# One decoder layer on one core: a norm weight spread by TensorE, two turns moved by a slot, two sample pieces moved, and the last sums divided among three engines

## The reference

```
h = RMSNorm(x) * norm_mix_pre
rq, rk, rv, rg, aq, ak, av, gr, ga = split(h @ w_in)
ret = retention(rotary(rq), rotary(rk), rv), per-head norm, times silu(rg)
att = dilated window attention in 3 groups over aq, ak, av (samples: over a cache)
mix = (sigmoid(gr) * (ret @ w_branch_ret) + sigmoid(ga) * (att @ w_branch_attn)) @ w_out
x = x + RMSNorm(mix) * norm_mix_post
f = (gelu(conv(h2 @ w_up)[g]) * conv(h2 @ w_up)[v]) @ w_down
y = x + RMSNorm(f) * norm_ffn_post
```

## Time and profile before

| what | value |
|---|---|
| runs | 1020.61, 1021.45 (median), 1021.92 us |
| the profiled execution | 1019.37 us, its span 1017.6 us |
| PE busy | 987.1 us, 97% of the span |
| DVE, ACT, POOL busy | 550.6, 380.0, 180.6 us |
| mean granted clock of TensorE | 0.994 |
| first product of a block | at 12.97 us |

### The profile page before, as it was taken

The page is one execution under the profiler, slowest core; times in us unless marked ns, Lnnn a source line. Parts: engine busy times, 40 slices in busy tenths (PEclk is TensorE's granted clock), DMA queues, the critical chain, the costliest instruction groups (busy, mean ns, idle before and its releaser), DMA issues.

```text
span 1017.6 us, 20374 instructions
## 1 busy us (share of the span) xinstructions
PE 987.1 (97%) x7774; PEld 877.5 (86%) x7774; DVE 550.6 (54%) x898; ACT 380.0 (37%) x836; POOL 180.6 (18%) x365
## 2 busy tenths in 40 slices
PE   6999999999999999999999889999999999999997
PEld 4777787779999999998887679999999999877775
DVE  5355225435367888773155576666666666422226
ACT  6333222441543423333133744444444443212313
POOL 2102004034161344445110001000010000000100
PEclk9999999999999999999999999999999999999999
DMA  6734444546796676769534324545545554221323
GB/s 240 275 121 153 167 174 166 189 153 207 257 300 220 194 234 203 240 198 320 187 120 137 123 76 156 179 172 167 188 170 174 165 176 143 84 83 63 120 83 117
DMA packets 40465, 175.36 MB, mean 172 GB/s; under 512 B 6936, under 2 KB 7384, under 8 KB 38864
## 3 DMA queue, kind: packets, MB, share of 16 engines
q1 hardware_dynamic: 25616, 125.78, 35.9%
q0 software_dynamic: 14784, 48.65, 15.2%
HBM read 164.40 MB, written 54.05 MB: 215 GB/s over the span
## 4 chain that ended last, share of the span: by engine, by line
PE 84%; DVE 8%; DMA 3%; ACT 2%; issue 2%; POOL 0%; SPq 0%; DVEq 0%; ACTq 0%
PE bank L1339 10%; PE bank L1341 9%; PE bank L1340 9%; PE bank L1847 9%; PE bank L1848 9%; PE bank L1849 9%; PE bank L1421 6%; PE bank L1425 5%; PE bank L1424 5%; PE bank L1358 2%; PE bank L1321 2%; DMA wraw<-in_weights 1%; DMA qbc<-sample_queries 1%; PE bank L1754 1%; DVE wlo L1932 1%
## 5 line engine op out<-in xcount | busy, mean ns | idle before, releaser
L1932 DVE TENSOR_TENSOR wlo<-wraw,whi 128x1024 fp32r<-128x1024 f32 x89 | 108.8, 1222 | 285.7 <-ACT whi L834 285.5
L834 ACT ACTIVATE whi<-wraw 128x1024 fp32r<-128x1024 f32 x91 | 96.3, 1058 | 318.5 <-PE bank L1341 204.9
L1847 PE MATMUL bank<-T1h,whi 128*128 128x288 f32 (+1 forms) x704 | 202.5, 288 | 3.1 <-DVE T1l L1942 1.7
L1848 PE MATMUL bank<-T1l,whi 128*128 128x288 f32 (+1 forms) x704 | 203.6, 289 | 0.0
L1849 PE MATMUL bank<-T1h,wlo 128*128 128x288 f32 (+1 forms) x704 | 203.1, 288 | 0.0
L1847 PEld LDWEIGHTS bank<-T1h,whi 128*128 128x128 f32 x704 | 133.0, 189 | 3.8 <-issue 1.9
L1848 PEld LDWEIGHTS bank<-T1l,whi 128*128 128x128 f32 x704 | 132.7, 189 | 0.0
L1849 PEld LDWEIGHTS bank<-T1h,wlo 128*128 128x128 f32 x704 | 132.3, 188 | 0.0
L1339 PE MATMUL bank<-whi,T1h 128*128 128x512 f32 (+1 forms) x288 | 114.0, 396 | 0.5 <-DVE T1l L1942 0.3
L1421 PE MATMUL bank<-T1h,whi 128*128 128x272 f32 x384 | 113.4, 295 | 0.0
L1425 PE MATMUL bank<-T1h,wlo 128*128 128x272 f32 x384 | 111.0, 289 | 0.0
(11 more groups left out here) (306 smaller groups left out, 1817.6 us busy)
## 6 DMA issues: line engine op xcount, KB each, us to landing
wraw<-in_weights SPq DMA_DIRECT2D x142, 512.0 KB, 3.7
out_s_kv_g<-in_cache_kv_g SPq DMA_DIRECT2D x64, 511.0 KB
qbc<-sample_queries POOLq DMA_DIRECT2D x48, 256.0 KB, 4.8
kvk<-in_cache_kv_g POOLq DMA_DIRECT2D x32, 256.0 KB, 4.0
kvv<-in_cache_kv_g POOLq DMA_DIRECT2D x16, 512.0 KB, 8.0
out_s_kv_g<-in_cache_kv_g SPq DMA_DIRECT2D x16, 508.0 KB
S<-in_state_ret POOLq DMA_DIRECT2D x16, 256.0 KB, 3.3
out_s_ret<-S POOLq DMA_DIRECT2D x16, 256.0 KB, 6.3
```

What stands on the lines that cost most here:

```text
L834: nc.scalar.activation(w_halves(s)[0], wraw[:, s % 2, :], ACT.Copy).then_inc(w_hi, 1)
L1847: mm(dst, Wh, T1h[:, k, c], start=k == 0, stop=False)
L1848: mm(dst, Wh, T1l[:, k, c], start=False, stop=False)
L1932: v.tensor_tensor(lo, wraw[:, s % 2, :], hi.bitcast(F), ALU.subtract).then_inc(w_lo, 1)
```

## The change

Four edits. (1) The norm weight is loaded as one row `grow` of 4 KB. PE multiplies a column of ones with it, two products of 512 columns in fp32 into banks 0 and 1. DVE copies these into `gpre`, and POOL, ahead of its two subtractions, waits for the products, since `grow` and `ones` lie where `wlo` will be. (2) `TURN_STEP` puts the turns of blocks 1 and 2 behind slot 2 rather than slot 1, on PE, ACT and DVE. (3) Two sample pieces go from the last two slots of the output gate to the first two of the retention gate; POOL now waits for output-gate slot 15 before it loads the near values. (4) For the first three tiles of the end, ACT scales the first half-row and POOL adds the residual, DVE does the second half alone.

```
-        sp.dma_start(gpre[:], a["norm_mix_pre"].broadcast_to([128, D])).then_inc(gpre_in, 16)
+        sp.dma_start(grow[0:1, :], a["norm_mix_pre"]).then_inc(grow_in, 16)
...
+        nc.gpsimd.memset(ones[0:1, :], 1.0).then_inc(ones_ready, 1)
...
+        pool.wait_ge(gain_full, 1)
         for j in range(2):
             pool.wait_ge(w_hi, j + 1)
...
+        pe.wait_ge(ones_ready, 1)
+        pe.wait_ge(grow_in, 16)
+        for half in range(2):
+            last = mm(P[half][:, :], ones[0:1, :], grow[0:1, 512 * half:512 * half + 512], start=True, stop=True)
+        last.then_inc(gain_full, 1)
         pe.wait_ge(ident_in, 16)
...
-        dve.wait_ge(gpre_in, 16)
+        dve.wait_ge(gain_full, 1)
+        for half in range(2):
+            v.tensor_copy(gpre[:, 512 * half:512 * half + 512], P[half][:, :]).then_inc(gpre_in, 1)
+        dve.wait_ge(gpre_in, 2)
...
+TURN_STEP = {1: 2, 2: 2, 5: 1, 6: 1, 7: 1}
...
-                turned = s == 1 and bi in (1, 2, 5, 6, 7)
+                turned = s == TURN_STEP.get(bi)
...
-                if bi in (1, 2) and s == 1:
+                if bi in (1, 2) and s == TURN_STEP[bi]:
                     turn_block(bi - 1)
...
-                if s == 1 and bi in (1, 2, 5, 6, 7):
+                if s == TURN_STEP.get(bi):
                     turn_evac(bi - 1, 1)
                     turn_evac(bi - 1, 3)
...
-PIECES_RG = 8 * (1,)
-PIECES_GB = 8 * (3, 2)
+PIECES_RG = (2, 2, 1, 1, 1, 1, 1, 1)
+PIECES_GB = 7 * (3, 2) + (2, 1)
...
         pool.wait_ge(s_step, 48)
+        pool.wait_ge(w_used, S_GB + 16)
         load_near_values(0)
-        pool.wait_ge(w_used, S_GB + 16)
...
+SHARED_LAST = 3
...
+        for p, i in enumerate(LAST_ORDER[:SHARED_LAST]):
+            r = rows(i)
+            pool.wait_ge(y_scaled, p + 1)
+            nc.gpsimd.tensor_tensor(fo[0:r, i, 0:512], fo[0:r, i, 0:512], xo[0:r, i, 0:512], ALU.add).then_inc(y_first, 1)
...
+                if 0 < p <= SHARED_LAST:
+                    i = LAST_ORDER[p - 1]
+                    r = rows(i)
+                    act.wait_ge(y_rs, p)
+                    nc.scalar.activation(x[0:r, i, 0:512], x[0:r, i, 0:512], ACT.Copy, scale=rs_n[0:r, at_ + i:at_ + i + 1]
+                                         ).then_inc(y_scaled, 1)
...
-            step(v.reciprocal(rs, rt_n[0:r, 10 + i:11 + i]))
-            for half in range(2):
+            v.reciprocal(rs, rt_n[0:r, 10 + i:11 + i]).then_inc(y_rs, 1)
+            dve.wait_ge(y_rs, p + 1)
+            for half in (1,) if p < SHARED_LAST else (1, 0):
```

More of the change, by code:

```diff
@@ L299, in build_layer @@
     gpre = sb("gpre", ATT + 5120, [128, D])
+    grow, ones = sb("gain_row", 13312 + SLOT, [128, D]), sb("ones", 13312, [128, 128])
     xn = sb("xn", ATT + 6144, [128, 2, D])
@@ L423, in build_layer @@
     x_again = [sem(f"x_again{i}") for i in range(TILES)]
-    ident_in = sem("ident_in")
+    ident_in, grow_in, ones_ready, gain_full = sem("ident_in"), sem("grow_in"), sem("ones_ready"), sem("gain_full")
     ca_in, cr_in, gpre_in, convp_in = sem("ca_in"), sem("cr_in"), sem("gpre_in"), sem("convp_in")
@@ L462, in build_layer @@
     half_sq, half_bias, x_scaled = sem("half_sq"), sem("half_bias"), sem("x_scaled")
-    y_sq, y_rt, y_ready = sem("y_sq"), sem("y_rt"), sem("y_ready")
+    y_sq, y_rt, y_rs, y_scaled = sem("y_sq"), sem("y_rt"), sem("y_rs"), sem("y_scaled")
+    y_first, y_ready = sem("y_first"), sem("y_ready")
     y_out = sem("y_out")
@@ L586, in _ @@
             dst = o["y_prompt"][0, 128 * i:128 * i + 128, :] if i < 4 else o["y_sample"].rearrange("b t d -> (b t) d")
-            parts = ((0, 512), (512, 1024)) if p == TILES - 1 else ((0, 1024),)
-            for c0, c1 in parts:
-                sp.wait_ge(y_ready, 2 * p + c1 // 512)
+            parts = ((512, 1024), (0, 512)) if p == TILES - 1 else ((0, 1024),)
+            for n, (c0, c1) in enumerate(parts):
+                if p < SHARED_LAST:
+                    sp.wait_ge(y_first, p + 1)
+                    sp.wait_ge(y_ready, p + 1)
+                else:
+                    sp.wait_ge(y_ready, 2 * p + 2 - SHARED_LAST - (len(parts) - 1 - n))
                 sp.dma_start(dst[:, c0:c1], fo[0:rows(i), i, c0:c1]).then_inc(y_out, 16)
```

## The result

The changed kernel took 1024.37 us (median of 19 runs, 1021.82 to 1027.34), the kernel before on the same chips 1020.40 us (19 runs): ratio 1.0043, 95% interval 1.0035 to 1.0051. It is slower by 0.43%, about 4 us. The forecast was 1024.7, and slower by over 0.2% the likeliest case. The total is right, but several of its terms are not, and a part of the agreement is luck.

The account below looks back on a forecast made before the run. PE was 97% busy, so only its waits, start and end counted. Terms +2.4 + 0.1 - 1.6 + 3.5 - 1.1 = +3.3 gave 1022.7 from the profiled 1019.37; adding its 2.1 us under the median gave 1024.7, range 1020.0 to 1027.4.

Parts of the forecast that it names:

- forecast +2.4: Start: the chain of row, two PE products and two DVE copies delays `xn`, costing 2.4 us.
- upper bound of 3.1: Start: the loss if all of the delay of `gpre` is carried to PE's products, +3.1 us.
- second rival: Start costs little, +0.9 us or less, by PE's fast pace and an early row; total 1023.2; chance 0.14.
- forecast +0.1: Turns of blocks 1 and 2: the wait on turned tiles is exchanged for one on `wlo`; +0.1 us for both.
- third rival: Turns of blocks 1 and 2 gain what they seem to, -2.6 us; total 1022.0; chance 0.06.
- forecast -1.6 and +3.5: Sample pieces: the `sTk` wait at the output gate's end goes, -1.6 us; PE's turn in the retention gate moves +3.5.
- the landing is later: Retention gate: piece 3's queries land 6.1 us after issue, at 301.25, later than DVE's work would reach it, 300.4.
- 4 us which the forecast named as a sign: Retention gate: the forecast would be wrong if piece 3's queries land within 4 us.
- forecast's own lower bound: Retention gate: the work alone, without a later landing of queries, delays PE's turn by +2.7 us.
- first rival: Retention gate: piece 3 holds nobody, so the 3.5 us go; total 1021.2, not slower; chance 0.20.
- forecast -1.07: End: without one half-sum in each of three tiles DVE finishes near 1014.03 instead of 1015.10, -1.07 us.
- fourth rival: End: POOL's third sum holds a DVE half-sum by up to 1.25 us; +0.8 us, total 1025.5; chance 0.10.

Follow-up runs that it names:

- experiment with the row first: Kernel before with only the norm-weight row change, the row's load issued ahead of x tile 0; ratio 0.9981 (0.9968 to 0.9994).
- Edit 2 alone: Kernel before with only the turns of blocks 1 and 2 moved behind slot 2; ratio 1.0013 (1.0000 to 1.0025).
- the split inside the rotation: Kernel before with the moved turns, DVE making `wlo` of slots 6 and 10 between third and fourth rotated tile; ratio 0.9971.
- edit 3 alone: Kernel before with only the two sample pieces moved to the first two retention-gate slots; ratio 1.0007 (0.9997 to 1.0017).
- two slots later: Kernel before with the two sample pieces moved to retention-gate slots 4 and 5 instead of 0 and 1; ratio 0.9971 (0.9957 to 0.9985).
- edit 4 alone: Kernel before with only the end's first three tiles shared with ACT and POOL; ratio 0.9986 (0.9974 to 0.9998).
- Sharing two tiles: Kernel before with only the end's change, two tiles shared with ACT and POOL instead of three; ratio 0.9990 (0.9979 to 1.0002).
- changed kernel with the row first: The whole changed kernel with the norm-weight row's load issued ahead of x tile 0; 1020.98 us, ratio 1.0003 to the kernel before.

## Why the prediction was right, and where not

The number was right: +3.3 forecast, +4.0 measured between medians, sign and range as forecast. A part of that is luck. The terms were counted from one profiled execution to another, and between the two profiles they come to +7.2: nearly every term of loss was too small, and the gain at the end too large. The 2.1 us that were then added, the distance of that execution from the median of three runs, are 1.0 by the median of 19. The four edits measured alone add up to +0.21 + 0.13 + 0.07 - 0.14 = +0.27%, about 2.8 us and uncertain by some 2.4, which agrees with 4.0 and is too coarse to check the sum.

Two of the forecast's bounds do not follow from their own terms: 2.4 less 1.1 or 1.6 is +1.3 or +0.8, not +0.9 for either, and 1024.7 + 1.8 + 0.7 is 1027.2, not 1027.4. Neither matters for the outcome.

**Edit 1, forecast +2.4.** The size is right and its making is not. Measured: ratio 1.0021, 2.1 us; by the sample rows' products 2.7 us against the mean of the old starts. The row landed at 4.6 (4.4 forecast), the products took 3.75 us (3.3), the first `xn` began at 9.93 (9.3 to 9.6), all near. But the first block product came at 16.18, outside the 14.5 to 15.3, and 3.2 us behind that of before, just past the upper bound of 3.1. The missing piece is the second `xn`: I gave it 1.48 us with its reciprocal, but its delay pushed it onto POOL's subtraction. The row for it was in the earlier trace rows, 1.94 us for 1.28, and I used it at the end of the kernel and not at the start. The experiment with the row first removes the overlap and the delay together, so their shares are read from the traces, not from a run that parts them. The forecast had POOL's part end near 11.3; it ended at 10.51 + 2.92 = 13.43, and the second `xn`, begun at 11.32, ran into it.

The second rival (the row near 3.3 by the Trainium skill, "DMA: Bandwidth & Descriptors", "Anatomy of one DMA") was wrong as placed: behind the 512 KB of x tile 0 the row landed with it. Alone in front it was in use 1.56 us after its issue at 0.74, somewhat less than that section's fixed cost of about 2 us; the section gives it for transfers that GpSimd issues, and this row went by SP, so the two need not agree. Nor did the queue become shorter by what the forecast said: with 4 KB in place of 512 KB, x tile 1 was squared at 7.73 and 7.93. In the seven profiles with the old start that was at 7.70 (the kernel before) and at 8.16 to 8.44 (the other six), 8.19 on average, so the tile came about 0.4 us sooner and not 1.7. Weight slot 0 was rounded at 9.32 in after, against 9.08 before; the forecast had that start near 7.4.

**Edit 2, forecast +0.1.** Shown right in mechanism: two waits of 1.5 us on `wlo` for two of 1.3 on the turned tiles. The size is +0.43 for each block, by the times at which PE starts the same products in the two traces. Of that 0.27 is that five tiles' turns took 2.37 us and not 2.1; the rest is not resolved. Edit 2 alone gave +1.3 us with an interval from 0 to 2.6. The third rival (a gain of 2.6) fell, and the run with the split inside the rotation shows what it lacked.

**Edit 3, forecast -1.6 and +3.5.** The gain at the gate's end is there: the wait on `sTk` is gone, 1.8 us by the same products. At the front the step that failed is "the landing is later". Piece 3's queries, issued at 299.75, landed 3.7 us later and not 6.1, at 303.45, which is 1.5 us before the piece began (304.98). That is within the 4 us which the forecast named as a sign that it would be wrong. It was wrong about what holds the chain; the hold itself came all the same, from the work. The wait for queries fell on piece 1 (0.91 us, about the 1 us given). The work alone bound it, the forecast's own lower bound: `w_split` started at 306.31 instead of 299.13, 7.2 us later, while PE came to its turn only 4.5 us later (310.17 - 2.96 = 307.21 against 303.00 - 0.29 = 302.71). The 2.7 us between them are what PE waits more: 2.96 for 0.29. What made the total larger again is a term that I did not have: the clock fell to 0.50 behind the wait, for 1.5 us more by the times of the same products. 2.7 + 1.5 = 4.2 us in these two profiles, against 3.5. That the two lie near each other is accident. The first rival, that piece 3 holds nobody, is refuted by the wait of 2.9 us in the run of edit 3 alone and by its absence two slots later.

**Edit 4, forecast -1.07.** Half of it came: 3.12 - 2.64 = 0.48 us, and the traces of three and of two shared tiles agree. The times alone (0.2 to 2.6 us for edit 4 alone) could not tell 0.5 from 1.07. The fourth rival's mechanism was there, since the half-sums took 2.15 us instead of 1.41. By the Trainium skill, "SBUF — State Buffer", "Who interferes with whom", a DVE instruction with two SBUF inputs and a POOL one that reads SBUF contend; the traces agree here and in the start (3.18 us for 1.28). Its price over the forecast is 2.64 - 2.05 = 0.6 us, and in after's trace that is all that was missing: half-sums of 1.41 us would have ended at 1017.90 + 1.41 = 1019.31, just as the last tile's square was done (1019.33), and they ended at 1020.05. Sharing two tiles does not reach the 2.05 (2.56), because DVE then carries the third tile's other half. Whether three sums by an engine that doesn't block DVE would reach 2.05 wasn't tried.

**The sum of the two profiles.** After less before, by the times at which PE starts the same products: start +3.4, first weight loads +0.3, turns 2 x 0.43, retention gate +4.2, one slot of the output gate +0.5, `sTk` -1.8, `hn`'s turns +0.35, end -0.5. Together 7.3, where the spans differ by 7.2. The medians differ by 3.2 less. Of the 19 runs of after, the 12 with a mean granted clock of 0.995 or more took 1024.0 us on average and the 7 with 0.994 or less 1026.2, so a part of that gap goes with the clock, and another 0.6 us with the lucky start of before's profile. The rest is open.

## What to carry to other kernels

When a wait is removed, write down what is late next and amend that too: three of these edits were a small loss or nothing as made, and a gain of 2 to 3 us once one thing more was moved. Put a tiny transfer that heads a chain ahead of the large ones, not behind. Before delaying a DVE instruction with two SBUF inputs, look at what POOL will be doing at its new time; and a wait of 0.3 us on a chain is a warning that the chain has no slack.

## What the hardware did that was not expected

- A PE wait of 2.2 to 3.0 us in the middle of dense work was followed by a granted clock of 0.50 for 2 us and more, in after, in edit 3 alone and in the changed kernel with the row first. Where the wait was 0.3 us at the same place the clock stayed at 1.00. The wait's price was half again as large as its row says, or more: by the stretches at most 1.7 us was lost behind each.
- The length of a wait does not settle this by itself. During or behind the wait of 3.1 us on `hn`, near 585 us, the clock fell to 0.50 in all ten profiles that have that wait, the kernel before among them; 1.7 us were lost in four (edit 2 alone, edit 4 alone, edit 1 with the row first, edit 3 two slots later) and 3.4 us in six. Behind the wait on `sTk` it fell, with 1.7 us lost, in the three profiles of edit 1, edit 2 and edit 4 alone, where PE waited 1.2 to 1.3 us, and not in the four others with that wait, where it was 1.6 us (the kernel before), 1.5 (the split inside the rotation), 1.0 and 0.9. So two single executions can differ by 1.7 us at a place that no edit touched, and to remove a wait can give back more than its row says. None of the five profiles without the `sTk` wait lost clock there. That would fit the 2.9 us of the pieces moved later, but no run shows it.
- At the start the granted clock reads 1.00 in every stretch while PE goes at half pace: before, 8 transposes took 1.94 us at 7.74 and 1.04 us at 594.83. The slow start can't be seen in that column.
- A 4 KB row issued 0.45 us after a 512 KB tile landed with it, at 4.58; issued before it, it was in use at 2.30. And taking 508 KB out of the queue behind x tile 0 brought the next tile only some 0.4 us sooner (7.73 and 7.93 against 8.19 on average), while with the row first it came at 6.51 to 6.83. Why is open: no run changes the transfer's size at a fixed place.
- Two fp32 products of 512 columns took 3.75 us at the start although they are one row deep: a broadcast by PE is not free there. The DMA of 512 KB that it replaced took 1.76 us.
